# Conformer layer: the sample tokens' depthwise convolution goes from VectorE to GpSimd, and in seven of eight chunks two prompt taps go from TensorE to VectorE

## The reference, cut to what matters

```python
def causal_depthwise(x_ext, w, b):
    y = conv_general_dilated(x_ext, w[:, None, :], window_strides=(1,), padding='VALID', ...,
                             feature_group_count=c)
    return y + b

def conformer_mixer(xn, conv_buf, w_pw1, b_pw1, dw_w, dw_b, ln_g, ln_b, w_pw2, b_pw2):
    p = xn @ w_pw1 + b_pw1
    z = p[..., :D_CONV] * sigmoid(p[..., D_CONV:])
    z_ext = concatenate([conv_buf, z], axis=1)        # 30 older rows before the new ones
    c = causal_depthwise(z_ext, dw_w, dw_b)           # 31 taps, per channel
    c = silu(layernorm(c, ln_g, ln_b))
    return c @ w_pw2 + b_pw2, z_ext[:, -30:]
```

## Time and profile before

| | |
|---|---|
| median of 3 runs | 2061.26 us (2058.8 to 2061.39) |
| profiled execution | 2061.06 us, of which the span of instructions is 2059.2 us |
| busy time: PE, DVE, ACT, POOL | 2011.5, 1544.0, 959.6, 784.4 us |
| granted TensorE clock over the span | 0.993 of full speed |
| Conformer convolution stage | about 1027 to 1131 us of the span |

### The profile page before, as it was taken

The page is one execution under the profiler, slowest core; times in us unless marked ns, Lnnn a source line. Parts: engine busy times, 40 slices in busy tenths (PEclk is TensorE's granted clock), DMA queues, the critical chain, the costliest instruction groups (busy, mean ns, idle before and its releaser), DMA issues.

```text
span 2059.2 us, 37564 instructions
## 1 busy us (share of the span) xinstructions
PE 2011.5 (98%) x14922; PEld 1852.2 (90%) x14922; DVE 1544.0 (75%) x2886; ACT 959.6 (47%) x1642; POOL 784.4 (38%) x502
## 2 busy tenths in 40 slices
PE   8999999999999999999998999999999999999998
PEld 7899999999889988887897999999998899888886
DVE  7868996555676578878699879975556766679886
ACT  5654453434444444444655654443434434444443
POOL 1014027777730055642110050088787400456420
PEclk9999999999999999999999999999999999999999
DMA  6684556676765568996422444566667655578973
GB/s 224 211 315 152 168 160 152 156 150 151 183 184 163 178 197 271 329 340 222 133 92 69 128 134 153 174 150 149 157 151 171 182 171 177 190 265 295 326 257 102
DMA packets 165918, 387.68 MB, mean 188 GB/s; under 512 B 55920, under 2 KB 78704, under 8 KB 163440
## 3 DMA queue, kind: packets, MB, share of 16 engines
q1 hardware_dynamic: 113712, 332.58, 49.4%
q0 software_dynamic: 49152, 33.75, 10.4%
q10 hardware_dynamic: 2880, 18.96, 2.3%
HBM read 361.67 MB, written 23.54 MB: 187 GB/s over the span
## 4 chain that ended last, share of the span: by engine, by line
PE 81%; DVE 14%; issue 2%; DMA 2%; ACT 2%; SPq 0%; DVEq 0%; ACTq 0%
PE ps L942 15%; PE ps L944 14%; PE ps L943 14%; PE ps L973 11%; PE ps L975 10%; PE ps L974 10%; PE ps L1020 4%; DVE w_lo L1534 2%; DMA land<-stream_dram 2%; DVE work L1420 2%; ACT w_hi L632 1%; DVE hidden L1420 1%; DVE hidden L1555 0%; DVE hidden L1546 0%; DVE work L1428 0%
## 5 line engine op out<-in xcount | busy, mean ns | idle before, releaser
L1534 DVE TENSOR_TENSOR w_lo<-land,w_hi 128x1024 fp32r<-128x1024 f32 x562 | 686.1, 1221 | 357.1 <-ACT w_hi L632 356.0
L942 PE MATMUL ps<-act_hi,w_hi 128*128 128x288 f32 x2688 | 808.6, 301 | 13.6 <-DVE act_lo L1260 4.8
L632 ACT CAST w_hi<-land 128x1024 fp32r<-128x1024 f32 x592 | 621.5, 1050 | 419.6 <-PE ps L975 299.5
L943 PE MATMUL ps<-act_hi,w_lo 128*128 128x288 f32 x2688 | 795.2, 296 | 0.0
L944 PE MATMUL ps<-act_lo,w_hi 128*128 128x288 f32 x2688 | 792.3, 295 | 0.0
L548 POOL DMA_INDIRECT gates_d<-rstd x256 | 452.6, 1768 | 320.1 <-DVE rstd L1687 193.4
L942 PEld LDWEIGHTS ps<-act_hi,w_hi 128*128 128x128 f32 x2688 | 506.0, 188 | 20.1 <-issue 8.9
L944 PEld LDWEIGHTS ps<-act_lo,w_hi 128*128 128x128 f32 x2688 | 508.1, 189 | 0.0
L943 PEld LDWEIGHTS ps<-act_hi,w_lo 128*128 128x128 f32 x2688 | 507.1, 189 | 1.0
L973 PE MATMUL ps<-w_hi,g_hi 128*128 128x512 f32 x1024 | 403.3, 394 | 5.7 <-DVE g_lo L1839 5.7
L974 PE MATMUL ps<-w_lo,g_hi 128*128 128x512 f32 x1024 | 399.7, 390 | 0.0
(11 more groups left out here) (223 smaller groups left out, 1497.0 us busy)
## 6 DMA issues: line engine op xcount, KB each, us to landing
land<-stream_dram SPq DMA_DIRECT2D x592, 512.0 KB
gates_d<-hidden ACTq DMA_DIRECT2D x16, 1024.0 KB, 5.9
work<-gates_d SPq DMA_DIRECT2D x96, 128.0 KB, 4.5
act_d<-smp_stage SPq DMA_DIRECT2D x64, 64.0 KB
gates_d<-rstd POOLq DMA_INDIRECT x256
hidden<-stream_dram,smp_idx POOLq DMA_INDIRECT x128, 5.9
x<-x_dram SPq DMA_DIRECT2D x4, 288.0 KB, 5.2
y_t_dram<-hidden SPq DMA_DIRECT2D x8, 144.0 KB, 1.9
```

Source lines behind the costliest of these rows:

```text
L632: nc.scalar.copy(w_hi[:, m, :], land[:, n % LANDS, :]).then_inc(w_hi_ready, 1)
L942: nc.tensor.matmul(out, w_hi[:, slot, wsl], hi, start=start, stop=False)
L943: nc.tensor.matmul(out, w_lo[:, slot, wsl], hi, start=False, stop=False)
L1534: V.tensor_tensor(w_lo[:, k, :], land[:, n % LANDS, :], w_hi[:, k, :].bitcast(F32), ALU.subtract).then_inc(lo_by_dve, 1)
```

## The change

The product of the sample convolution is made by GpSimd, and so is the sum: not a reduction but a tree of additions in place, that halves the row of 34 (34, 17, 9, 5, 3, 2) and ends with a seventh instruction and the bias. Each of these instructions waits for the one before it by the semaphore `conv_step`. The copy to `packs[c]` stands behind them. VectorE loses its three instructions per chunk. `TAPS` becomes 12 in chunks 0 to 6, so that VectorE has two taps more in each of these; chunk 7 keeps 22. `centre` and the first column sum wait for the new semaphore `smp_conv`.

```diff
-TAPS = (14, 14, 14, 14, 14, 14, 14, 22)
+TAPS = (12, 12, 12, 12, 12, 12, 12, 22)
...
                     for c in range(CH):
                         pool.wait_ge(evacuated[1], USES + USE_IN + c + 1)
+                        shape = [P, NSEQ, SL, ZROW]
+                        samples = z_ext[:, c, ZEXT_S:ZEXT].rearrange("p (s w) -> p s w", s=NSEQ)
+                        sums = cv[:, c, TP:T].rearrange("p (s w) -> p s w", s=NSEQ)
+                        nc.gpsimd.tensor_tensor(conv_prod, samples.unsqueeze(2).to_broadcast(shape),
+                                                wide_w[:, c, :, :].unsqueeze(1).to_broadcast(shape),
+                                                ALU.mult).then_inc(conv_step, 1)
+                        width, made = ZROW, 2
+                        while width > 2:
+                            half = width // 2
+                            pool.wait_ge(conv_step, 7 * c + made - 1)
+                            nc.gpsimd.tensor_tensor(conv_prod[:, :, :, 0:half], conv_prod[:, :, :, 0:half],
+                                                    conv_prod[:, :, :, width - half:width],
+                                                    ALU.add).then_inc(conv_step, 1)
+                            width, made = width - half, made + 1
+                        pool.wait_ge(conv_step, 7 * c + 6)
+                        nc.gpsimd.tensor_tensor(sums, conv_prod[:, :, :, 0], conv_prod[:, :, :, 1],
+                                                ALU.add).then_inc(conv_step, 1)
+                        pool.wait_ge(conv_step, 7 * c + 7)
+                        nc.gpsimd.tensor_scalar(cv[:, c, TP:T], cv[:, c, TP:T], col("cf_dw_b", c), None,
+                                                ALU.add).then_inc(smp_conv, 1)
+                        if c < CH - 1:
+                            pool.wait_ge(smp_conv, c + 1)
                         nc.gpsimd.tensor_copy(packs[c], z_ext[:, c, ZEXT_S:ZEXT].rearrange(
...
                     if L == 1 and n == 2 * PIVOT + 5:
+                        pe.wait_ge(smp_conv, PIVOT)
                         column_sum(cv, cv_ready, 0, ACC, PIVOT)
...
                 def conv(c):
...
-                    shape = [P, NSEQ, SL, ZROW]
-                    did(V.tensor_tensor(conv_prod, seqs(z_ext[:, c, ZEXT_S:ZEXT]).unsqueeze(2).to_broadcast(shape),
-                                        wide_w[:, c, :, :].unsqueeze(1).to_broadcast(shape), ALU.mult))
-                    products = steps[0]
...
-                    dve.wait_ge(step, products)
-                    did(V.tensor_reduce(seqs(cv[:, c, TP:T]), conv_prod, AX_X, ALU.add))
...
-                    did(V.tensor_scalar(cv[:, c, TP:T], cv[:, c, TP:T], col("cf_dw_b", c), None, ALU.add))
...
                     dve.wait_ge(cv_ready, c + 1)
+                    dve.wait_ge(smp_conv, c + 1)
                     V.tensor_tensor(cv[:, c, :], cv[:, c, :], pivot, ALU.subtract).then_inc(centred, 1)
```

More of the change, by code:

```diff
@@ L414, in build @@
         wide_ready = sem("wide_ready")
+        conv_step = sem("conv_step")
+        smp_conv = sem("smp_conv")
         gate_scaled = sem("gate_scaled")
@@ L1469, in conformer @@
                 split_lo(SLABS + IN0 + 1 + LEAD)
-                dve.wait_ge(wide_ready, 1 + SL)
                 gate_in(1)
```

## The result

The changed kernel takes 2073.45 us (median of 6 runs, 2071.12 to 2074.31) beside 2060.2 us for the kernel before (6 runs, 2058.8 to 2061.39): a ratio of 1.0061 [1.0048, 1.0074], slower by 10 to 15 us. The prediction had +19.3 us, 2080, with a range of 2070 to 2100.

A forecast was written before the change was run, and what follows sets the result against it. VectorE was taken to bound the Conformer convolution stage. Work removed, -20.6, taps added, +5.6, and GpSimd's chain, +32.2 in seven chunks and +2.1 in chunk 0, summed to +19.3 us: 2080 us, range 2070 to 2100.

The forecast's parts named there:

- What left and what came to VectorE: Convolution stage: product, reduction and bias leave VectorE, -20.6 us; two more taps in each of seven chunks, +5.6 us.
- the price of the chain: Chunks 1 to 7: GpSimd's eight new instructions hold up VectorE for 4.6 us per chunk, 32.2 us in all.
- the price per element: GpSimd's two-operand instructions: each element costs VectorE 2.08 ns, so 2144 elements cost 4.46 us per chunk.
- The 0.14 us added for the bias and for short instructions: GpSimd's chain: the state copy's price, added per chunk for the bias and short instructions' cost beyond their elements.
- 3.9, if only the long ones cost anything: Lower bound of the chain's price per chunk: only the three long instructions cost, 1888 elements at 2.08 ns.
- Chunk 0: First chunk's chain: partly in VectorE's idle time, it eats ScalarE's 0.6 us gain and costs 2.1 us.
- Engines apart: Rival, convolution stage: GpSimd and VectorE do not hold each other up, -15.6 us, 2045 us; chance 0.06.
- Strided access: Rival, GpSimd's chain: strided operands cost more, 2090 us for the tree alone, 2100 for all; chance 0.15.
- Whole instructions block: Rival, GpSimd's chain: each of eight instructions costs a fixed 0.25 us more, 13 us in all, 2093 us; chance 0.08.
- Short ones free: Rival, GpSimd's chain: 3.9 us per chunk, 2075 us or as low as 2068; chance 0.10 for below 2072.
- The clock: Rival, convolution stage: TensorE, idling 4.4 us per chunk, falls to 1.2 GHz, over 2110 us; chance 0.03.
- The waits added: State copy and SyncE's store behind GpSimd's chain: the waits cost 0, or about a microsecond in chunk 0.

The follow-up runs named there:

- the memsets: The changed kernel with GpSimd's product, tree and bias replaced by 15 memsets per chunk that only write: 2047.99 us, ratio 0.9935.
- the copies: The changed kernel with each chunk's seven two-operand GpSimd instructions replaced by one-operand copies of the same shapes: 2059.25 us, ratio 0.9988.
- taps-only kernel: The kernel before with TAPS at 12 in seven chunks and nothing else: 2064.41 us, ratio 1.0017.
- GpSimd-alone kernel: The changed kernel with TAPS back at 14, so only the sample convolution moves: 2067.8 us, ratio 1.0035.

## Why the prediction was right, and one term too large

**The bound and the mechanism held.** VectorE sets the stage before and after; the stage alone moved; a waiting GpSimd instruction gets in behind VectorE's current one and holds the next. That it is GpSimd's reading, and not its presence, is shown by the memsets (no cost) against the copies (1.6 us per chunk) and the two-operand chain (3.85). The Trainium skill says the same on who meets whom (SBUF — State Buffer, "Who interferes with whom": a two-input VectorE instruction contends with a GpSimd instruction that reads SBUF, not with one that only writes it), and the traces agree, with taps of 0.48 us (median) beside 5.96 us of memsets.

**What left and what came to VectorE** held: 2.58 us less and, in the taps-only kernel, 0.81 more per chunk (0.80 predicted). In time that kernel came out at +3.0 us where its terms give 5.6, the end of its interval.

**The mis-sized term is the price of the chain**, 32.2 us for seven chunks at 4.6. Measured are 3.85 us, so 7 x 0.75 = 5.2 us of the 6.5 by which the stage's 12.77 falls short of 19.3. The step that failed is the price per element: 2.08 ns was measured on the subtraction of slabs and carried over to another operation. The product shows 1.91, the first halving 1.71. With it went GpSimd's own duration: the prediction scaled the slab's 2.39 us up to 2.5 for the product, which took 2.30. The 0.14 us added for the bias and for short instructions did not show either: the pieces listed above come to 3.8 us without it. The bound of "3.9, if only the long ones cost anything" was the right number for another reason: short instructions cost too, 0.22 us for 128 elements and 0.08 for 64, but every one costs less per element than the slab's. So the time came near the forecast by a right mechanism with a price a fifth too high, inside a range that allowed for it.

**Chunk 0** was put at 2.1 us. From its L1439 to that of chunk 1 there are 4.96 us now and were 4.67; the next interval grew by 2.66, 0.6 more than the later ones (2.07). So it cost about 0.9 us, and the remaining 1.2 us of the error lies here. That less of the chain met VectorE's two-input work than I took is the likely reason; it was not measured apart.

**The rivals.** *Engines apart* is refuted by the 2.55 us tap, and what it would have been worth was measured: -13.4 us with memsets, near the -15.6 worked out. The TensorE lead that was to "just hold" there did not. *Strided access* did not show: the halvings, with runs of 17 and less, cost less per element than the product. *Whole instructions block* would have cost 4.6 + 1.86 = 6.5 us per chunk; measured are 3.85. It was close for a single long instruction, though: the product, 2.30 us beside an idle VectorE in chunk 0, held a tap for 2.08 us in the later chunks, and the others above fall short of their duration by the same quarter of a microsecond. For the halvings no undisturbed duration is on record; their records, own waits in them, are 1.25, 0.76, 0.54 and 0.40 us, and cost 0.93, 0.44, 0.22 and 0.08. By the rule of the Trainium skill that the prediction cites (SBUF — State Buffer, stated in full in its section "SBUF: two separate sides") each would cost its whole duration; the measurement decides: about 0.2 us less for the product. *Short ones free* is refuted by the same rows (0.44, 0.22 and 0.08 us), though its time of 2068 to 2075 holds the result. *The clock*: the prediction named a clock below 1.00 in the stage as a sign that it was wrong. It did fall, to 1.2 GHz behind waits of 2.80 and 8.56 us, and that sign was badly chosen: VectorE never waited for TensorE in the stage, and the price is the same 3.88 us in a period of the GpSimd-alone kernel at 1.00. That the clock would add nothing to the time was right, but the argument for it rested in part on a misread row: the wait ahead of the stretch with 0.91 is shorter than the 3.15 us over which the clock stayed at 1.00, not longer. TensorE's timeline before:

```profile
1131.55 1.32 PE L1157 MATMUL ps<-hidden,ones 128*128 128x288 f32 x2 [2.72 <-DVE hidden L1464]
```

**The waits added** cost nothing that the trace shows. In SyncE's timeline the store of chunk 1's state, which now stands behind the whole chain, follows 0.04 us after the end of two slab loads that stretch over 10.56 us; the queue waits at the loads, not at the store. In chunk 0 the store did wait for the chain: it goes out at 1033.53, 0.03 us after GpSimd's copy. But the next load, at 1034.62, follows the end of VectorE's `w_lo` (1033.17 + 1.42 us) by 0.03 us, so that was the wait that ended last for it.

```profile
1034.62 10.56 SPq L470 DMA_DIRECT2D land<-stream_dram  x2
1045.22 0.43 SPq L480 DMA_DIRECT2D cfs_t_dram<-hidden  x1
```

**What should show it** did: six side taps of 6.20 us (some 6 predicted), taps of 2.5 us and more (2.55), GpSimd busy 7.6 us per period (8 predicted), waits of TensorE of 1.8 to 3.4 us in four chunks and one of 8.56, where some 4 in each chunk were predicted. The period is 15.20, where 15.95 was predicted.

## What to carry to other kernels

GpSimd is no free engine beside a VectorE that is the bound and reads two SBUF tensors: each element of a long two-operand GpSimd instruction cost VectorE 1.6 to 2.1 ns here, and VectorE itself took 1.10 ns for an element of the product (1.20 us for 1088); with its two taps the move could only pay below 2.0 us per chunk, and only the memsets and the one-operand copies (1.6 us) were below. A price per element is taken from the operation nearest in operands and layout; if it must come from another, the price there and GpSimd's own duration for the new shape bound it better than one figure alone. What did pay, 4.5 us, was taking work off VectorE: a tap per chunk to TensorE, up to the point where TensorE's own period was as long, the bias into an instruction that was there, and the state copies to ScalarE. These three were not run apart.

## What the runs showed of the hardware that I had not expected

- GpSimd's price for VectorE per element: nothing for memsets, about 0.75 ns for copies from one operand, 1.6 for a subtraction of one contiguous buffer from itself, 1.9 for the product with its two broadcast operands. The slab's subtraction has 2.08, unexplained. Five undisturbed durations on GpSimd, from 0.38 to 2.39 us, are about 0.25 us longer than what the instruction cost.
- A VectorE product of 992 elements took 2.0 us with one operand eight elements apart, and 1.18 us with a contiguous copy of it, with the same overlapping windows as the other.
- TensorE came back to a granted clock of 0.50 after a wait of 8.56 us and stood at 1.00 again some 6 us later, with no cost here.
